# Raw key and query products of five chunk pairs kept in DRAM and read back when the scan meets the pairs again

## The reference

```python
gc = jnp.cumsum(g, axis=-1)
decay = jnp.where(incl, jnp.exp(jnp.where(incl, diff, 0.0)), 0.0)
kb = k * beta[..., None]
m = jnp.where(strict, jnp.einsum('bhncd,bhnsd->bhncs', kb, k) * decay, 0.0)
a = m + jnp.eye(DN_CHUNK, dtype=m.dtype)
...
attn = jnp.where(incl, jnp.einsum('bhncd,bhnsd->bhncs', q, k) * decay, 0.0)
...
o_b, s_b = gated_delta_chunked(flip(q), flip(k), flip(v), flip(g[:, :, 1]), flip(beta[:, :, 1]), s0_b)
```

## Time and profile before

| | |
|---|---|
| median of 3 runs | 3622.85 us (3619.99 to 3624.35) |
| the profiled execution | 3618.07 us, its span 3616.3 us |
| TensorE busy over the span | 3426.3 us (95%) |
| VectorE, ScalarE, GpSimd busy | 1749.9, 1016.2, 796.7 us |
| steps 0 to 17 of the scan | about 696 to 1045 us of the span |
| mean granted TensorE clock | 0.970 of full speed |

### The profile page before, as it was taken

The page is one execution under the profiler, slowest core; times in us unless marked ns, Lnnn a source line. Parts: engine busy times, 40 slices in busy tenths (PEclk is TensorE's granted clock), DMA queues, the critical chain, the costliest instruction groups (busy, mean ns, idle before and its releaser), DMA issues. The chain is left out here.

```text
span 3616.3 us, 40963 instructions
## 1 busy us (share of the span) xinstructions
PE 3426.3 (95%) x15380; PEld 2161.2 (60%) x15380; DVE 1749.9 (48%) x2647; ACT 1016.2 (28%) x2101; POOL 796.7 (22%) x784
## 2 busy tenths in 40 slices
PE   6999999799989996899999999999879999999998
PEld 2445444799964444444444444445567878878786
DVE  4454545566656534532223222234366665666666
ACT  3365565455544111311111111122201111111113
POOL 1022222355536000101111111123312122111211
PEclk9999999899999998999999999999879999999999
DMA  8222322788655118721111311144416666656566
GB/s 298 74 73 84 102 79 76 233 252 254 214 180 178 47 47 275 259 66 58 41 58 58 108 46 59 35 161 146 158 60 240 215 198 215 196 196 221 180 206 256
DMA packets 370877, 533.65 MB, mean 148 GB/s; under 512 B 61357, under 2 KB 237328, under 8 KB 370490
## 3 DMA queue, kind: packets, MB, share of 16 engines
q1 hardware_dynamic: 347364, 472.32, 39.1%
q0 software_dynamic: 12096, 43.84, 4.6%
q10 hardware_dynamic: 11221, 14.87, 1.1%
HBM read 420.94 MB, written 112.13 MB: 147 GB/s over the span
## 5 line engine op out<-in xcount | busy, mean ns | idle before, releaser
L2887 POOL TENSOR_TENSOR mg<-mg,sg_m 128x512 f32<-128x512 f32 x64 | 98.1, 1533 | 778.3 <-DVE sg_m L2768 778.3
L3774 PE MATMUL bank<-xeT,raw_e 128*128 128x128 f32 x2304 | 268.0, 275 | 0.8 <-ACT xeT L3618 0.8
L3774 PEld LDWEIGHTS bank<-xeT,raw_e 128*128 128x128 f32 x2304 | 263.6, 192 | 8.3 <-issue 8.3
L2674 PE MATMUL bank<-hT,raw_w 128*128 128x512 f32 x576 | 261.9, 598 | 5.2 <-PEq L2478 5.2
L992 POOL TENSOR_SCALAR sg<-tmp 128x512 f32<-128x512 f32 (+1 forms) x76 | 113.4, 1492 | 438.4 <-DVE tmp L1060 368.5
L2674 PEld LDWEIGHTS bank<-hT,raw_w 128*128 128x128 f32 x576 | 110.7, 192 | 144.0 <-issue 144.0
L3774 PE MATMUL bank<-T_e,U 128*128 128x128 f32 x1536 | 176.8, 275 | 0.0
L3774 PEld LDWEIGHTS bank<-T_e,U 128*128 128x128 f32 x1536 | 174.1, 192 | 0.0
L2674 PE MATMUL bank<-zT,S 128*128 128x512 f32 x384 | 172.6, 592 | 0.0
L698 PE MATMUL bank<-T_d,S_d 128*128 128x512 f32 x384 | 171.5, 593 | 0.0
L2737 ACT ACTIVATE sg_m<-sg_m 128x512 f32<-128x512 f32 x72 | 45.4, 630 | 395.0 <-DVE sg_m L2777 395.0
(11 more groups left out here) (542 smaller groups left out, 6894.4 us busy)
## 6 DMA issues: line engine op xcount, KB each, us to landing
raw_e<-in_exp_w_gate SPq DMA_DIRECT2D x16, 3072.0 KB, 16.4
raw_e<-in_exp_w_up SPq DMA_DIRECT2D x16, 3072.0 KB, 12.9
raw_e<-in_exp_w_down SPq DMA_DIRECT2D x16, 3072.0 KB, 10.3
raw_w<-in_w_in SPq DMA_DIRECT2D x24, 1024.0 KB, 5.6
raw_d<-in_w_in SPq DMA_DIRECT2D x16, 1024.0 KB, 5.8
raw_h<-in_w_in SPq DMA_DIRECT2D x12, 1024.0 KB, 5.3
x0T<-in_ada_w SPq DMA_DIRECT2D x44, 256.0 KB, 3.3
raw_h<-kT_d SPq DMA_DIRECT2D x36, 256.0 KB, 5.9
```

The source lines that it names most:

```text
L2674: mm = pe.matmul(bank[:, :], lhs[:, k, :], rhs[:, k, :], start=first and k == 0, stop=k == 3, skip_group_check=not first)
L2887: pool.tensor_tensor(mg[:, i, :], mg[:, i, :], sg[:, i, :], ALU.add).then_inc(add_ok[i], 1)
L3774: mm = pe.matmul(bank[:, f * P:(f + 1) * P], lhs[:, k, f * P:(f + 1) * P], rhs[:, k, :], start=fresh and k == 0, stop=k == 3, skip_group_c ...
```

## The change

Fronts 4 to 8 (`KEPT`) make their raw products as before, and ScalarE copies each out of PSUM bank 3: key products by two copies of 128x256 into small buffers (`key_copied`), query products by one copy of 128x512 over the queries in `qF` (`query_copied`). `gram` and `attention` of these fronts wait for the copies (`kept_ok`) and read them in place of PSUM. SyncE stores the copies in two new DRAM tensors. Fronts 11 to 15 (`AGAIN`) load these tensors in place of keys and queries, have no `key_product` and no `query_product`, and let `gram` and `attention` read the loaded products. Fronts 9, 10, 16 and 17 stay as they are. The order of the operations on VectorE is unchanged.

The diff, cut to its core:

```diff
+            KEPT, AGAIN = range(AHEAD, NCH // 2 - 1), range(NCH // 2 + 1, NCH - AHEAD)
+            keysA, keysB = sbt(st, "keysA", [P, HEADS, P]), sbt(st, "keysB", [P, 2, P])
+            formed = lambda f, d: 2 * sum(1 for v in range(f) if v not in AGAIN) + d + 1
+            copied = lambda f, i: KEPT0 + 4 * (f - AHEAD) + i
...
                     def load_front(f):
-                        if f >= 2:
-                            sp.wait_ge(kq_mm, nth(f - 2, 1))
+                        if f - 2 in AGAIN or f - 2 in KEPT:
+                            sp.wait_ge(at_ok, nth(f - 2, 1))
+                        elif f >= 2:
+                            sp.wait_ge(kq_mm, formed(f - 2, 1))
+                        if f - 2 in KEPT:
+                            sp.wait_ge(kq_st, kq_stored(f - 2))
...
+                            sp.dma_start(kF[:, f % 2, d], chunked(kk_d if f in AGAIN else kT_d, f, d)).then_inc(ldf[f % 2], 16)
...
+                    def store_key_products(f):
+                        for d in range(2):
+                            sp.wait_ge(kept_ok, copied(f, d + 1))
+                            for part, h in kk_parts[d]:
+                                sp.dma_start(chunked(kk_d, f, d)[:, h:h + 2], part).then_inc(kk_st, 16)
+                    def store_query_products(f):
+                        for d in range(2):
+                            sp.wait_ge(kept_ok, copied(f, d + 3))
+                            sp.dma_start(chunked(kq_d, f, d), qF[:, f % 2, d]).then_inc(kq_st, 16)
...
                         if s >= 1:
                             store_output(s - 1)
+                        if s + AHEAD - 1 in KEPT:
+                            store_query_products(s + AHEAD - 1)
...
                             store_gram(s + AHEAD)
+                        if s + AHEAD in KEPT:
+                            store_key_products(s + AHEAD)
...
+                        elif f in KEPT:
+                            pe.wait_ge(kept_ok, copied(f, 1))
+                        elif f in KEPT:
+                            pe.wait_ge(kept_ok, copied(f, d + 2))
...
-                        if ahead:
+                        if ahead and f not in AGAIN:
                             key_product(f, 0)
...
+                    def key_copied(f, d):
+                        act.wait_ge(kk_mm, formed(f, d))
+                        if f > AHEAD:
+                            act.wait_ge(n_ok, nth(f - 1, d))
+                        if d == 0 and f > AHEAD:
+                            act.wait_ge(kk_st, kk_stored(f - 1))
+                        for part, h in kk_parts[d]:
+                            last = act.activation(part, b4(3)[:, h:h + 2], ACT.Copy)
+                        last.then_inc(kept_ok, 1)
+                    def query_copied(f, d):
+                        act.wait_ge(kq_mm, formed(f, d))
+                        act.activation(qF[:, f % 2, d], b4(3), ACT.Copy).then_inc(kept_ok, 1)
...
                         f, m = s + AHEAD, s + 1
+                        if f - 1 in KEPT:
+                            query_copied(f - 1, 1)
...
                             for l in range(1, NL):
+                                if f in KEPT:
+                                    key_copied(f, l - 1)
                                 other_halves(m, l)
                                 turned(m, l)
+                            if f in KEPT:
+                                query_copied(f, 0)
...
+                        if f in AGAIN:
+                            dve.wait_ge(ldf[f % 2], 64 * (f // 2 + 1))
+                        elif f in KEPT:
+                            dve.wait_ge(kept_ok, copied(f, d + 1))
...
+                        products = [kF[:, f % 2, d, h] if f in AGAIN else kk_parts[d][h // 2][0][:, h % 2] if f in KEPT else b4(front_bank(f, 1 + d))[:, h, :] for h in heads]
...
                     def attention(f, d):
+                        if f in KEPT:
+                            dve.wait_ge(kept_ok, copied(f, d + 3))
```

More of the change, by code:

```diff
@@ L134, in build @@
     o_d = [scr(n, (NCH, P, HEADS, P)) for n in ("of_d", "ob_d")]
+    kk_d, kq_d = [scr(n, (NCH, P, HEADS, P)) for n in ("kk_d", "kq_d")]
     nc_d, ti_d = scr("nc_d", (STEPS, 32 * BLK)), scr("ti_d", (4, 64 * BLK))
@@ L1198, in build @@
             prod, unit = sbt(st, "prod", [P, 64]), shared[:, 1024:1280]
+            KEPT, AGAIN = range(AHEAD, NCH // 2 - 1), range(NCH // 2 + 1, NCH - AHEAD)
+            keysA, keysB = sbt(st, "keysA", [P, HEADS, P]), sbt(st, "keysB", [P, 2, P])
+            kk_parts = [[(keysA[:, 0:2], 0), (keysA[:, 2:4], 2)], [(aff.rearrange("p a b -> p (a b)").rearrange("p (h t) -> p h t", t=P), 0), (keysB[:, :, :], 2)]]
+            kept_ok, KEPT0 = m_tr, 4
+            kk_st, kq_st, ST0 = x_in[0], x_in[1], 16
             ldf, ldk, ldv, o_st = [[sem(f"{name}{r}") for r in range(2)] for name in ("ldf", "ldk", "ldv", "o_st")]
@@ L1217, in build @@
             nth = lambda s, d: 2 * s + d + 1
+            formed = lambda f, d: 2 * sum(1 for v in range(f) if v not in AGAIN) + d + 1
+            copied = lambda f, i: KEPT0 + 4 * (f - AHEAD) + i
+            kk_stored = lambda f: ST0 + 64 * (f - AHEAD + 1)
+            kq_stored = lambda f: ST0 + 32 * (f - AHEAD + 1)
             level = lambda m, l: NL * m + l + 1
@@ L1280, in load_front @@
                         for d in range(2):
-                            sp.dma_start(qF[:, f % 2, d], chunked(qT_d, f, d)).then_inc(ldf[f % 2], 16)
+                            sp.dma_start(qF[:, f % 2, d], chunked(kq_d if f in AGAIN else qT_d, f, d)).then_inc(ldf[f % 2], 16)
                     def sums_of(f, d):
@@ L1393, in _ @@
                                 c0 = B_OFF + q * HW
-                                sp.wait_ge(kq_mm, nth(STEPS - 1, 1))
+                                sp.wait_ge(kq_mm, formed(STEPS - 1, 1))
                                 sp.dma_start(raw_h[:, q], A["w_in"][0, :, c0:c0 + HW].rearrange("(k p) c -> p k c", p=P)).then_inc(raw_h_in, 16)
@@ L1418, in key_product @@
                             pe.wait_ge(n_ok, nth(f // 2, d))
+                        elif d == 0 and f - 1 in KEPT:
+                            pe.wait_ge(kept_ok, copied(f - 1, 4))
                         elif d == 0:
                             pe.wait_ge(at_ok, nth(f - 1, 1))
+                        elif f in KEPT:
+                            pe.wait_ge(kept_ok, copied(f, 1))
                         else:
@@ L1668, in gram @@
                     def gram(f, d):
-                        dve.wait_ge(kk_mm, nth(f, d))
+                        if f in AGAIN:
+                            dve.wait_ge(ldf[f % 2], 64 * (f // 2 + 1))
+                        elif f in KEPT:
+                            dve.wait_ge(kept_ok, copied(f, d + 1))
+                        else:
+                            dve.wait_ge(kk_mm, formed(f, d))
                         dve.wait_ge(Em_ok, nth(f, d))
@@ L1674, in gram @@
                         dst = N2[:, :, :] if d else Nc[:, f % AHEAD]
+                        products = [kF[:, f % 2, d, h] if f in AGAIN else kk_parts[d][h // 2][0][:, h % 2] if f in KEPT else b4(front_bank(f, 1 + d))[:, h, :] for h in heads]
                         for h in heads:
-                            last = dve.scalar_tensor_tensor(dst[:, h, :], attn(f, d)[:, h, :], column(beta, f, d, h), b4(front_bank(f, 1 + d))[:, h, :], ALU.mult, ALU.mult)
+                            last = dve.scalar_tensor_tensor(dst[:, h, :], attn(f, d)[:, h, :], column(beta, f, d, h), products[h], ALU.mult, ALU.mult)
                         last.then_inc(n_ok, 1)
@@ L1683, in attention @@
                     def attention(f, d):
-                        dve.wait_ge(kq_mm, nth(f, d))
-                        dve.tensor_tensor(attn(f, d), attn(f, d), b4(front_bank(f, 3 + d)), ALU.mult).then_inc(at_ok, 1)
+                        if f in KEPT:
+                            dve.wait_ge(kept_ok, copied(f, d + 3))
+                        elif f not in AGAIN:
+                            dve.wait_ge(kq_mm, formed(f, d))
+                        dve.tensor_tensor(attn(f, d), attn(f, d), qF[:, f % 2, d] if f in KEPT or f in AGAIN else b4(front_bank(f, 3 + d)), ALU.mult).then_inc(at_ok, 1)
                     def rest(s, d):
```

3 lines of the change are left out of this document (2 added, 1 removed).

## The result

| | before | after |
|---|---|---|
| median of 5 runs | 3622.85 us | 3657.49 us |
| ratio, with its 95% interval | | 1.0096 (1.0083 to 1.011) |
| profiled execution | 3618.07 us | 3659.65 us |
| steps 0 to 4 (fronts 4 to 8) | 102.12 us | 141.74 us |
| steps 5 and 6 | 40.67 us | 40.59 us |

What follows compares the result with a forecast made beforehand. TensorE was taken to bound the scan. Stalls +24, turns with GpSimd +9, late fronts -1 and transfers zero gave +32 us; on the median before of 3622.85 that is 3655 us, range 3637 to 3675.

Steps and rivals of the forecast that it cites:

- First stall: Fronts 4 to 8: gram 1 waits for ScalarE's key copy behind turned 1, delaying crossed 1 and outer 1; 2.4 us TensorE idle.
- The cover of key copy 0: Fronts 4 to 8: the copy of key product 0 still lets joined 0 end before inner 1 wants it, by 0.2 us.
- Second stall: Fronts 4 to 8: attention 0 waits for query copy 0 behind turned 2, delaying crossed 2 and outer 2; another 2.4 us.
- Turns: Grams of fronts 4 to 8, both inputs in SBUF, alternate instruction by instruction with GpSimd; +9 us, bounds 0 and 21.
- The clock: TensorE's clock in the scan was taken to stay at 1.00, so the main forecast gave it no term.
- a sign that it is wrong: The prediction is wrong if, among other signs, the clock leaves 1.00 in the scan.
- a rival with 0.17: Steps 0 to 4: idle time ahead of outer 1 lowers the clock, +8.5 us or more, 3663 to 3672 us; chance 0.17.
- Late fronts: Fronts 11 to 15: fewer TensorE products, but VectorE's gram and attention still hold crossed; -1 us, bounds -10.3 and +5.
- the losses of even steps: Steps 8 and 10: gram 0, gram 1 and gram sum or attention lose 3 us to GpSimd against 1.7 saved.
- the inverse's way: Late fronts: the inverse's path through GpSimd and DRAM was claimed to get no shorter; no separate size given.
- Transfers: Steps with added stores, 4 x 256 KB each: no delay expected, zero; at the upper end 1 us a step, +5.

Runs made afterwards that it cites:

- the kernel that reads PSUM: Against the changed kernel, gram and attention of fronts 4 to 8 read products from PSUM, still waiting for the copies: 3642.85 us, ratio 1.0069.

## Why the prediction came out near, and where it was wrong

- **First stall, 2.4 us a step.** Right in place and cause; in the kernel that reads PSUM, without turns, it is 2.10 us. The two key copies took 0.65 us, not 0.73. In the changed kernel it is 2.12 to 4.04 us, with the turns in it. The cover of key copy 0, put at 0.2 us, failed once: in step 0 joined 0 came late and TensorE waited 2.75 us.
- **Second stall, 2.4 us.** Right in place and about in size: 1.18 + 0.77 us of TensorE idle in step 2, after a copy of 0.59 us. That query product 1 fits in front held, but it has a wait of its own, 1.18 us, and outer 2 only the 0.77 behind it. Both together were put at 24 us and measured 22.1.
- **Turns, +9 us.** Measured 8.0, partly by luck: the forecast had 2.3 us in each even step and 1.0 in each odd one, measured by step are 4.7, 0.1, 0.9, 1.6 and 0.8, with a small part of the clock in them. The reading of whole instructions taken in turns held: a gram went from 1.12 to 2.2 us in step 2 here and to 4.15 us when each of its four instructions met one of GpSimd. What the Trainium skill states (SBUF — State Buffer, Who interferes with whom), that such instructions exclude each other for their whole length, agrees with these numbers.
- **The clock, 0 in the sum.** This step failed. The clock fell in all five steps, 0.88 to 0.94, which the prediction itself names as a sign that it is wrong. In the kernel that reads PSUM it cost 9.5 us. I held it for a rival with 0.17, whose price of 8.5 us was near, and gave it a wrong condition. From one row behind 2.33 us of idle with no loss I took it that a stretch of 2.4 us is harmless. The kernel that reads PSUM lost its clock with no stretch over 2.10 us. Nor does the length of a stretch decide: a single one of 1.99 us cost part of the clock, a single one of 3.02 us nothing, and the pair of 2.10 and 1.99 us nothing in step 0 but something in steps 1 to 4. What decides is not shown by these runs; that the clock stays when the stretches are filled is.
- **Late fronts, -1 us.** Measured -3.2. The direction of even and odd was right (19.96 and 20.90 against 18.87, 19.46 and 19.05), the losses of even steps were put too high, 21.6 us. That the inverse's way gets no shorter was right, and it is a limit close behind; what holds TensorE in the changed kernel itself are joined and crossed.
- **Transfers, 0.** Right for this kernel, and for the reason given: the steps were longer, and the inverse came in time. As soon as the waits were taken away it was wrong, with up to 6 us in one step.
- **Sum.** +32 was forecast. From it to the +36.1 of the scan: +9.5 clock, -1.9 waits, -1.0 turns, -2.2 late fronts, -0.3 elsewhere; of these only the clock is larger than what steps of the same code differ by. The total came out near 3655 because errors of both signs met. The cause of most of it, the order of the copies, is shown by the two kernels that move them.

No version beats the kernel before. The one with the copies behind gram and attention can't be told from it by its total, though its scan is 5.3 us longer.

## What to carry to other kernels

Saving work on the bounding engine is worth only what the next chain leaves: here 16 products of a head less gave 0.6 us of a step of 20.3, since TensorE then waited for VectorE's work of the front, and behind that stood a solve through DRAM at nearly the same length. A copy that is to be kept for later belongs behind the consumers that are waited for, not in front of them, and ahead of no instruction of a chain that crosses engines. And give the clock a term of its own as soon as a change leaves TensorE idle for some 2 us at a time: here such stretches cost nothing in some steps and over 2 us beyond their length in others (28.14 against 24.88).

## What the runs showed of the hardware

The clock fell to 1.2 GHz in steps whose only idle stretches were 2.10 and 1.99 us, with TensorE busy for the rest of the step, and stayed at 2.4 GHz when useless matmuls cut them to 0.32 and 0.20 us; the difference was 9.5 us in five steps. It fell behind a single stretch of 1.99 us in one kernel and stayed at 2.4 GHz behind a single one of 3.02 us in another. Four VectorE instructions of 0.34 us with both inputs in SBUF took 4.15 us together while GpSimd worked: each ended some 0.15 us after a whole GpSimd instruction, three of which were of 128x512 and took 1.08 to 1.31 us.
